# Down projection of the feed-forward: four buffers of sums, an early load of four pairs' weights, and the last two pairs taken product by product

## What is computed

```python
def conv_ffn(h, w_up, conv_w, conv_b, w_down):
    u = h @ w_up                                  # 512 x 1024 by 1024 x 5504
    c = conv_b + conv_w[0] * up[:, 0:S] + ...     # causal convolution of three taps over the rows
    gate, val = jnp.split(c, 2, axis=-1)
    return (jax.nn.silu(gate) * val) @ w_down     # 512 x 2752 by 2752 x 1024

x = x + conv_ffn(h, ...)
```

## Time and profile before

| | us |
|---|---|
| median of 3 runs | 1441.59 |
| lowest, highest | 1437.18, 1444.06 |
| the profiled execution, its own time | 1443.28 |
| its span, first to last instruction | 1441.1 |
| PE busy in the span | 1381.0 (96%) |
| mean granted clock of TensorE | 0.978 of full |

### The profile page before, as it was taken

The page is one execution under the profiler, slowest core; times in us unless marked ns, Lnnn a source line. Parts: engine busy times, 40 slices in busy tenths (PEclk is TensorE's granted clock), DMA queues, the critical chain, the costliest instruction groups (busy, mean ns, idle before and its releaser), DMA issues.

```text
span 1441.1 us, 16083 instructions
## 1 busy us (share of the span) xinstructions
PE 1381.0 (96%) x5860; PEld 866.9 (60%) x5860; DVE 787.2 (55%) x1915; ACT 351.4 (24%) x859; POOL 259.9 (18%) x261
## 2 busy tenths in 40 slices
PE   3898979999999999999999999999999999999997
PEld 3444555544544544655455566444588888888786
DVE  5867699428633363113555666113567776774544
ACT  5122211214400002111355666010022323220000
POOL 1068467204202186600000000000000000000000
PEclk8897989999999999999999999999999999999999
DMA  9582134423303112300301001120331323231320
GB/s 306 202 158 83 34 106 134 144 87 125 140 7 106 59 59 59 117 30 10 137 1 60 1 1 59 37 81 0 102 116 60 110 66 107 70 106 51 117 70 30
DMA packets 85769, 120.58 MB, mean 84 GB/s; under 512 B 15256, under 2 KB 43230, under 8 KB 85692
## 3 DMA queue, kind: packets, MB, share of 16 engines
q1 hardware_dynamic: 80992, 110.80, 24.5%
q10 hardware_dynamic: 2956, 5.05, 1.1%
q0 software_dynamic: 1744, 3.70, 0.9%
HBM read 111.00 MB, written 6.84 MB: 82 GB/s over the span
## 4 chain that ended last, share of the span: by engine, by line
PE 85%; DVE 10%; issue 1%; SPq 1%; DMA 1%; ACT 1%; POOL 1%; DVEq 0%; ACTq 0%; POOLq 0%
PE bank L756 21%; PE bank L1291 17%; PE bank L1317 8%; PE bank L766 6%; PE bank L1202 6%; PE bank L784 5%; PE bank L1043 4%; PE bank L1158 3%; PE bank L1182 3%; PE bank L1261 2%; PE bank L1055 2%; PE bank L1011 1%; PE bank L1368 1%; DVE arena L2209 1%; PE bank L1140 1%
## 5 line engine op out<-in xcount | busy, mean ns | idle before, releaser
L756 PE MATMUL bank<-arena 128*128 128x512 f32 (+1 forms) x800 | 342.2, 586 | 2.0 <-ACT arena L1620 1.6
L756 PEld LDWEIGHTS bank<-arena 128*128 128x128 f32 x800 | 151.9, 193 | 173.9 <-issue 168.8
L1291 PE MATMUL bank<-arena 128*128 128x256 f32 x1120 | 242.0, 379 | 0.0
L1291 PEld LDWEIGHTS bank<-arena 128*128 128x128 f32 x1120 | 212.9, 190 | 29.5 <-issue 0.8
L784 PEld LDWEIGHTS bank<-arena 128*128 128x128 f32 (+2 forms) x692 | 84.3, 146 | 87.3 <-issue 47.6
L784 PE MATMUL bank<-arena 128*128 128x128 f32 (+2 forms) x692 | 98.8, 282 | 32.6 <-DVE arena L2225 7.6
L1317 PE MATMUL bank<-arena 128*128 128x256 f32 x560 | 125.0, 386 | 2.8 <-DVE arena L2685 2.1
L1317 PEld LDWEIGHTS bank<-arena 128*128 128x128 f32 x560 | 108.0, 194 | 19.5 <-DVE arena L2685 2.5
L766 PE MATMUL bank<-arena 128*128 128x512 f32 x256 | 113.0, 600 | 0.0
L1797 POOL TENSOR_TENSOR arena<-arena 128x1 f32<-128x1 f32 x8 | 4.4, 554 | 476.7 <-DVE arena L1998 476.7
L2514 DVE CUSTOM_DVE_ANT_0 arena<-bank,arena 128x128 f32<-128x128 f32 (+3 forms) x128 | 57.7, 488 | 58.9 <-PE bank L1158 58.1
(11 more groups left out here) (345 smaller groups left out, 1717.4 us busy)
## 6 DMA issues: line engine op xcount, KB each, us to landing
arena<-in_w_in SPq DMA_DIRECT2D x14, 2048.0 KB, 7.8
arena<-in_w_up SPq DMA_DIRECT2D x20, 1024.0 KB, 6.8
arena<-in_w_ada SPq DMA_DIRECT2D x8, 1024.0 KB, 13.0
arena<-in_w_down SPq DMA_DIRECT2D x8, 1024.0 KB, 6.2
arena<-in_w_ada SPq DMA_DIRECT2D x2, 2048.0 KB, 8.3
arena<-in_w_out SPq DMA_DIRECT2D x2, 2048.0 KB, 7.8
arena<-in_w_attn_br SPq DMA_DIRECT2D x2, 2048.0 KB, 8.7
arena<-in_w_o SPq DMA_DIRECT2D x2, 2048.0 KB, 7.8
```

Of the source, the lines that this page charges most:

```text
L756: mm = pe.matmul(ps[:, 0:n], act[:, k, 128 * t:128 * t + 128], w[:, k, 0:n], start=(k == 0), stop=(k == kt - 1))
L1291: mm = pe.matmul(ps, left[:, k, :], right[:, k, :], start=(first and k == 0), stop=(k == 3), skip_group_check=True)
```

## The change

Three parts, and what goes with them.

1. **Four buffers of sums.** Two more buffers lie in the room of `wS`. `down_sums(n)` waits for pair n - 4 in place of n - 2.
2. **Chunk (1, 0), the weights of pairs 10 to 13, goes into `hT`.** SP issues it right behind chunk (0, 1), once the last group of the up projection has ended. The list of chunks loses that entry, so chunk (1, 1) now waits for pair 8 and chunk (1, 2) for pair 10, and both slots are one chunk further on. On DVE `down_sums(11)` now stands ahead of the first half's outputs.
3. **The last two pairs of the second half, product by product.** PE takes pairs 18 and 19 together: first P1, P5, P7, P6 for i = 0, then for i = 1; then for each i the left-over tiles of P2 and P3, P2, P3, the left-over tiles of P4 and R, P4. DVE does both first parts of the outputs (`down_first`, the first 8 operations), then both second parts (`down_second`, the last 4). `down_rest` now takes a pair of accumulators at a time, in both halves.

The number of matmuls, of DVE operations, of copies and of transfers stays the same.

```diff
+        WS0 = z.at
         wS = z.take(2 * 4 * 512, 2, 4, 4, 128)
...
+        dSb, dTb = [[b_[:, 0], b_[:, 1]] + [arena[:, WS0 + 2048 * a + o:WS0 + 2048 * a + o + 1024]
+                                            .rearrange("p (a b) -> p a b", a=4) for a in range(2)]
+                    for b_, o in ((dS, 0), (dT, 1024))]
...
+        DOWN_FIRST, DOWN_SECOND = ("P1", "P5", "P7", "P6"), ("P2", "P3", "P4")
+        DOWN_ENDS = [(0, i, name) for i in range(2) for name in DOWN_FIRST + DOWN_SECOND][:-1] + \
+            [(1, i, name) for names in (DOWN_FIRST, DOWN_SECOND) for i in range(2) for name in names]
+
+        def down_last(a, i, name):
+            return DOWN_ENDS.index((a, i, name)) + 1
...
-            for b in range(3):
+            for b in range(a, 3):
...
+            if name == ("d", 1, 0):
+                eng.wait_ge(d10_in, 32)
+                return hT
...
+            def down_rows(k, nk, a):
+
+                return w_down_2[0, 128 * k:128 * k + 128 * nk, 512 * a:512 * a + 512].rearrange("(k p) n -> p k n", p=128)
...
+                            sp_.dma_start(w[:, nk * h:nk * h + nk, :], down_rows(NP * h + 4 * b, nk, a))                               .then_inc(slot_full[n % 2], 16)
+                        if (a, b) == (0, 1):
+                            sp_.wait_ge(product_done, 7 * NG)
+                            for h in range(2):
+                                sp_.dma_start(hT[:, 4 * h:4 * h + 4, :], down_rows(NP * h, 4, 1)).then_inc(d10_in, 16)
...
-                if (i, name) == (1, "P4"):
+                if a == 0 and (i, name) == (1, "P4") or a and not last and (i, name) == (1, "P4"):
...
+            def down_views(a, p, i):
 
                 n, b = NP * a + p, p // 4
                 nk = 4 if b < 2 else 2
+                w = weights(pe, ("d", a, b))
+                kp, kq = p - 4 * b, nk + p - 4 * b
+                lo, hi = slice(128 * i, 128 * i + 128), slice(256 + 128 * i, 384 + 128 * i)
+                s_ = [dSb[n % 4][:, m, lo] for m in range(4)]
+                t_ = [dTb[n % 4][:, m, :] for m in range(4)]
+                return {"P1": (aT[:, p, lo], w[:, kp, 0:256]), "P5": (s_[0], t_[0]), "P7": (s_[2], t_[2]), "P6": (s_[1], t_[1]),
+                        "P2": (aT[:, p + NP, lo], w[:, kq, 0:256]), "P3": (s_[3], w[:, kq, 256:512]),
+                        "P4": (aT[:, p + NP, hi], t_[3])}
...
                 pe.wait_ge(dsum_done, n + 1)
...
-            def down_rest(a):
-
-                if a == 0:
+                    down_product(a, i, "P4", *view["P4"], first, last)
+
+            def down_rest(a, i, names, h):
+
+                w = weights(pe, ("d", a, 2))
+                for k, m in ((FT - 2, 128), (FT - 1, 64)):
+                    left = aT[0:m, k, 256 * h + 128 * i:256 * h + 128 * i + 128]
+                    for c, name in enumerate(names):
+                        pe.matmul(down_acc(i, name), left, w[0:m, k - FT + 6, 256 * c:256 * c + 256],
+                                  start=False, stop=(name == "R" and m == 64), skip_group_check=True)
+
+            for p in range(NP):
+                if p == 8:
                     pe.wait_ge(act_done, 2)
-                w = weights(pe, ("d", a, 2))
-                for i in range(2):
-                    for k, m in ((FT - 2, 128), (FT - 1, 64)):
-                        for h, names in enumerate((("P2", "P3"), ("P4", "R"))):
-                            left = aT[0:m, k, 256 * h + 128 * i:256 * h + 128 * i + 128]
-                            for c, name in enumerate(names):
-                                pe.matmul(down_acc(i, name), left, w[0:m, k - FT + 6, 256 * c:256 * c + 256],
-                                          start=False, stop=(name == "R" and m == 64),
-                                          skip_group_check=True)
-
-            for a in range(2):
-                for p in range(NP):
-                    if p == 8:
-                        down_rest(a)
-                    down_pair(a, p)
+                    for i in range(2):
+                        down_rest(0, i, ("P2", "P3"), 0)
+                        down_rest(0, i, ("P4", "R"), 1)
+                down_pair(0, p)
+            for p in range(NP - 2):
+                down_pair(1, p)
+            pe.wait_ge(dsum_done, 2 * NP)
+            ends = (NP - 2, NP - 1)
+            for i in range(2):
+                for name in DOWN_FIRST:
+                    for p in ends:
+                        down_product(1, i, name, *down_views(1, p, i)[name], False, p == NP - 1)
+            for i in range(2):
+                down_rest(1, i, ("P2", "P3"), 0)
+                for name in ("P2", "P3"):
+                    for p in ends:
+                        down_product(1, i, name, *down_views(1, p, i)[name], False, p == NP - 1)
+                down_rest(1, i, ("P4", "R"), 1)
+                for p in ends:
+                    down_product(1, i, "P4", *down_views(1, p, i)["P4"], False, p == NP - 1)
...
-                        act.wait_ge(dlast_done, 13 * a + 7 * i + (2, 2, 4)[n])
+                        act.wait_ge(dlast_done, down_last(a, i, ("P5", "P5", "P6")[n]))
...
-                if n >= 2:
-                    v.wait_ge(dpair_done, n - 1)
+                if n >= 4:
+                    v.wait_ge(dpair_done, n - 3)
...
-                s_ = [dS[:, n % 2, m, :] for m in range(4)]
-                t_ = [dT[:, n % 2, m, :] for m in range(4)]
+                s_ = [dSb[n % 4][:, m, :] for m in range(4)]
+                t_ = [dTb[n % 4][:, m, :] for m in range(4)]
...
+            def down_first(a, i):
...
-                v.wait_ge(dlast_done, n0 + 6)
+
+            def down_second(a, i):
+
+                (x11, x12), (x21, x22) = down_blocks(a, i)
+                v.wait_ge(dlast_done, down_last(a, i, "P3"))
                 v.scalar_tensor_tensor(x11, down_acc(i, "P2"), 0.5, x11, ALU.mult, ALU.add).then_inc(x3_done, 1)
                 v.scalar_tensor_tensor(x12, down_acc(i, "P3"), 0.5, x12, ALU.mult, ALU.add).then_inc(x3_done, 1)
-                if i:
-                    v.wait_ge(dpair_done, NP * a + NP)
+                if (a, i) == (0, 1):
+                    v.wait_ge(dpair_done, NP)
                 else:
-                    v.wait_ge(dlast_done, n0 + 7)
+                    v.wait_ge(dlast_done, down_last(a, i, "P4"))
                 v.scalar_tensor_tensor(x22, down_acc(i, "R"), 0.5, x22, ALU.mult, ALU.add).then_inc(x3_done, 1)
                 v.scalar_tensor_tensor(x21, down_acc(i, "P4"), 0.5, x21, ALU.mult, ALU.add).then_inc(x3_done, 1)
 
...
-            for n in range(2, NP + 1):
+            for n in range(2, NP + 2):
                 down_sums(n)
-            down_out(0, 0)
-            down_sums(NP + 1)
-            down_out(0, 1)
+            for i in range(2):
+                down_first(0, i)
+                down_second(0, i)
             for n in range(NP + 2, 2 * NP):
                 down_sums(n)
-            down_out(1, 0)
-            down_out(1, 1)
+            down_first(1, 0)
+            down_first(1, 1)
+            down_second(1, 0)
+            down_second(1, 1)
```

More of the change, by code:

```diff
@@ L551, in program @@
         dsum_done = sem("dsum_done")
+        d10_in = sem("d10_in")
         dpair_done = sem("dpair_done")
@@ L1336, in down_pair @@
                         pe.wait_ge(block_done, 4 * (NG - 2 + i) + 4)
-                    lo, hi = slice(128 * i, 128 * i + 128), slice(256 + 128 * i, 384 + 128 * i)
-                    A11, A12, A22 = aT[:, p, lo], aT[:, p + NP, lo], aT[:, p + NP, hi]
-                    s_ = [dS[:, n % 2, m, lo] for m in range(4)]
-                    t_ = [dT[:, n % 2, m, :] for m in range(4)]
-                    B11, B21, B22 = w[:, kp, 0:256], w[:, kq, 0:256], w[:, kq, 256:512]
+                    view = down_views(a, p, i)
@@ L1342, in down_pair @@
                     if first and a:
                         pe.wait_ge(dcopy_done, 3 * i + 2)
-                    down_product(a, i, "P1", A11, B11, first, last)
-                    down_product(a, i, "P5", s_[0], t_[0], first, last)
+                    down_product(a, i, "P1", *view["P1"], first, last)
+                    down_product(a, i, "P5", *view["P5"], first, last)
                     if first and a:
                         pe.wait_ge(du_done, i + 1)
-                    down_product(a, i, "P7", s_[2], t_[2], first, last)
@@ L1349, in down_pair @@
-                    down_product(a, i, "P6", s_[1], t_[1], first, last)
+                    down_product(a, i, "P7", *view["P7"], first, last)
+                    down_product(a, i, "P6", *view["P6"], first, last)
                     if first and a:
                         pe.wait_ge(x3_done, 4 * i + 2)
-                    down_product(a, i, "P2", A12, B21, first, last)
-                    down_product(a, i, "P3", s_[3], B22, first, last)
+                    down_product(a, i, "P2", *view["P2"], first, last)
@@ L1354, in down_pair @@
```

(9 more changed lines are left out.)

14 lines of the change are left out of this document (5 added, 9 removed).

## The result

| | before | changed |
|---|---|---|
| median, lowest and highest, us | 1436.89 (1435.09 to 1444.06), 8 runs | 1427.44 (1425.99 to 1433.38), 8 runs |
| profiled execution, its own time | 1443.28 | 1433.38 |
| its span | 1441.1 | 1431.4 |
| from the first matmul of the down projection to the span's end | 1441.1 - 1290.7 = 150.4 | 1431.4 - 1290.0 = 141.4 |

The ratio is 0.9925, with a 95% interval of 0.9904 to 0.9947: 0.75% faster by this ratio, which is 10.8 us; the two medians are 9.45 us apart.

A forecast was written before the change was run, and what follows sets the result against it. PE, busy 96% of the span, was taken to bound the kernel, leaving time only in its waits, low clock and the end. -6.28 + 0.3 + 1.5 - 4.34 = -8.8 us from 1441.59 gave 1432.8 us, range 1429.0 to 1437.5.

The forecast's parts named there:

- passage, taken away: Down projection, between output halves, pairs 10 and 11: PE's waits (3.87 us) and slow clock (2.4 us) go, -6.28 us.
- wait that stays at P2 of pair 10: Between the output halves: PE still waits for DVE's release of P2, +0.3 us, of 0 to 0.35.
- eight more changes of row count: Left-over tiles, both halves: eight more changes on PE at 0.19 us each, +1.5 us, bounds 0 and 2.6.
- DVE behind PE at the end: Program's end: DVE ends 0.9 us behind PE's last product where it was 5.24, -4.34 us.
- last transfer: Program's end: the 2.44 us from the last transfer's issue to the span's end stays, counted as nothing.
- What I costed at nothing: Down projection: load into `hT`, later `down_sums(12)`, chunks issued a step sooner, earlier output transfers; 0 us.
- the signs of being wrong: `x3_done` wait over 0.5 us at pair 10, clock falling behind 1290, or PE's last 88 records over 20.6 us.
- Rival A: Between the halves: the median run lacks the slow clock, so gain 6.4 us, time 1435.2; chance 0.30.
- Rival B: Between the halves: DVE's outputs start late, PE waits again and the clock may fall, time 1438.8; chance 0.07.
- Rival C: Last 88 records: eight 0.33 us stops bring the clock to 1.2 GHz, slower, up to 1451.8 us; chance 0.03.

The follow-up runs named there:

- the second profile: The kernel before, unchanged, profiled once more; 149.6 us from the first matmul of the down projection to the span's end.
- the passage alone: Parts 1 and 2 without part 3, left-over tiles and end as in the kernel before, against that kernel; ratio 0.9948, length 144.3 us.
- the experiment with two changes: The changed kernel with two changes of row count in each half in place of eight; length 139.1 us, 2.3 less than the changed kernel.
- the end alone: Part 3 on the kernel before, with two buffers, the old passage and weights of pairs 10 to 13 through slots; ratio 1.0008, length 152.8 us.

## Why the prediction was right or wrong

**The step that failed is the base and what I allowed for it, not the change.** I took the median of three runs, 1441.59, as the time from which the 8.8 us go off, and ended the range 3.8 us below 1432.8. This kernel's times lie in two groups some 6 us apart. Two of my three runs were of the upper one, but only three of the eight that the changed kernel was compared with, so their median is 1436.89, 4.7 us lower. The same 8.8 us taken from 1436.89 give 1428.1, against 1427.4 measured. Within the lower groups it was 1436.0 (5 of 8 runs) to 1426.8 (6 of 8): 9.2 us.

Nor would more runs alone have helped: the 35 later runs of the kernel before have a median of 1441.54, that of my three, because 22 of them were of the upper group. Where the groups are about equally full, the median goes from one to the other by the luck of the draw. Three runs that spread 6.9 us should have told me that the base may lie in either group, whatever the change does: the range had to reach down from the lowest run, 1437.18 - 8.8 = 1428.4, and below. I had used the spread on either side of the median alone.

**The sum, term by term**, against the first two profiles:

| term | forecast | measured |
|---|---|---|
| passage, taken away | -6.28 | -6.28 in the first profile of before, -5.4 in the second |
| wait that stays at P2 of pair 10 | +0.3 | +0.3 (idle 0.28) |
| eight more changes of row count | +1.5 | +1.6 |
| DVE behind PE at the end | -4.34 | -4.45 |
| last transfer | 0 | 0 (2.5 us behind DVE's end, as before) |
| sum | -8.8 | -8.9 by the terms, -9.0 by the lengths (150.4 to 141.4), -8.2 from the second profile |

With the passage alone it was 6.1 us less, where 6.0 were forecast. For the changes of row count: the first half's left-over tiles take 1346.71 - 1338.34 = 8.37 us where they took 7.58, and the end from 1414.30 to 1428.12 is 13.66 us of pace (less the 0.16 by which a record outlasts it) for 56 records, 12.08 at 0.2157: 1.6 us for eight changes, 0.2 each. Both agree with the 0.19 of the forecast, and so does the experiment with two changes (2.3 us for 12); the 0.163 of the Trainium skill's formulas (TensorE: Matmul & The Clock Gate, Part 2) is a little low.

**What I costed at nothing** was nothing: the load into `hT`, the lead of `down_sums`, the shifted slots. I had missed that the load is not needed at all, and that the new end stands on more than two buffers. One reading in the prediction was loose: ahead of the fall PE had been idle for the 2.08 us of the earlier trace rows, not for half a stretch.

Of the signs of being wrong that I had named none came: the wait at pair 10 is 0.28 us, the granted clock is 1.00 from 1290 to PE's end, and PE's last 88 records took 6.9 + 13.66 = 20.6 us, right at the bound.

**Rival A**, no slow clock in the typical passage, is not borne out: the clock fell there in all three profiled executions with the old passage (the two of before, and the end alone); runs without a profile can't be seen into. What varied is how long it stayed low. Its observation was right, that runs differ by some 6 us, but in the profiled executions that difference arises 1150 us ahead of the change. **Rival B**, a wait that stays, holds for 0.3 us only. **Rival C**, the clock falls at the end, did not come in the changed kernel; it came with the end alone, by another mechanism than I gave, a wait for sums and not the changes of row count. **That it got faster** by over 0.5% was right, and the forecast ratio of 0.9939 stands in the measured interval.

## What to carry to other kernels

When one engine's queue holds both the work that frees the accumulators and the work that prepares the next inputs, the bound is the order in that queue; buy just enough buffers to move the preparation ahead (here the fourth brings 0.7 us against three, and the early load nothing). A regrouping at the end of a program asks for its inputs earlier, so check how far ahead they can be made before pricing it. And forecast a difference from traces, but an absolute time only with a range that reaches into every group of the runs: here the median itself moved by 4.7 us with the share of each group, so compare group with group.

## What I had not expected of the hardware

- One stretch of lower clock, far from the change, goes with the group of an execution. In nine traces of twelve PE had waited 1.17 to 2.13 us for ACT near 131 us and then had 10 us or so at a clock down to 0.5; in the other three it had waited 0.16 us or not at all, and the clock stayed full. Near 148 us the two profiles of the changed kernel are 7.2 us apart. That the wait brings the clock down fits all twelve, but no run changed the wait alone; why it is there in only some executions stays open.
- The same wait of 2.08 us, with a second behind it, brought the clock down in three executions of three, but for 6.8 us in one profile of before and with the end alone (there 0.83, 0.50, 0.50, 0.50 and 0.97 in the stretches of 2 us from 1358), and for 3.4 us in the other profile of before; 2.4 us were lost by it in the first profile and 1.6 in the second. With 1.30 us in place of 2.08 the clock stayed at full, while near 131 us, behind other work, it fell after a wait of 1.17 us. The length of the wait alone does not tell.
- A lower clock around a wait can cost less than its length says. In the first profile of before it was low for 6.8 us, by the earlier trace rows and the two stretches between:

```profile
1366.00:1368.00 2.00, 1.29 (x4) 0.55 (x3) 1.93 (x6) 0.00 (x0) 0.00 (x0) 0.50 0.11 39
...
1370.00:1372.00 2.00, 2.00 (x6) 1.56 (x5) 1.64 (x5) 0.00 (x0) 0.00 (x0) 0.50 0.00 0
```

That would be 3.4 us of work, and it cost 2.4. As I read it, PE would have waited for part of that time anyway.
